# Modulation multiply-adds on VectorE: directly behind each step's weight residue instead of at the step's end

## The reference

```python
def modulation(cvec, w, b):
    return jnp.split(jax.nn.silu(cvec) @ w + b, 6, axis=-1)

    mx = modulation(c, ada_w[i], ada_b[i])
    mc = modulation(c_ctx, ada_w[i], ada_b[i])
    hx = modulate(rms_norm(x, norm_g[i, 0]), mx[0][:, None], mx[1][:, None])
...
    x = x + mx[2][:, None] * yx
    hx = modulate(rms_norm(x, norm_g[i, 1]), mx[3][:, None], mx[4][:, None])
...
    x = x + mx[5][:, None] * y[:b * s].reshape(b, s, d)
```

## Time and profile before

| | |
|---|---|
| median of 3 runs | 2205.7 us (2204.92 to 2208.37) |
| profiled execution, device time | 2208.73 us |
| its span, first to last instruction | 2207.2 us |
| TensorE busy (matmul) | 1989.5 us (90%) |
| VectorE busy | 1227.8 us (56%) |
| ScalarE busy | 496.2 us (22%) |
| mean granted TensorE clock | 0.956 of full |
| group 0, about | 136 to 236 us |
| groups 1 to 7, about | 236 to 1003 us |
| output projection, routing | 1003 to 1270 us |
| experts | 1270 to 2207 us |

### The profile page before, as it was taken

How to read it: one execution, slowest core, us unless ns; L and a number is a source line. 1 busy time by engine, 2 the same in 40 slices (tenths; PEclk the granted TensorE clock), 3 DMA queues, 4 the chain that set the end, 5 groups by cost and what they waited for, 6 DMA issues and landing times.

```text
span 2207.2 us, 27594 instructions
## 1 busy us (share of the span) xinstructions
PE 1989.5 (90%) x10090; PEld 1232.7 (56%) x10090; DVE 1227.8 (56%) x1999; ACT 496.2 (22%) x577; POOL 152.3 (7%) x214
## 2 busy tenths in 40 slices
PE   5778999999999999998999798998988999888988
PEld 2357777788787878786778533333333333333333
DVE  2456788888888888887786623332223333322224
ACT  3123333333333333334445300000000000000000
POOL 0000000000000000000592100000000000000000
PEclk9788999999999999999999899999999999999999
DMA  9958576767676767678663699999999999999997
GB/s 351 311 172 241 161 220 182 221 182 221 183 219 186 215 192 215 188 224 298 209 210 133 243 423 426 428 427 426 425 427 425 427 426 427 427 425 426 426 425 286
DMA packets 294717, 666.68 MB, mean 302 GB/s; under 512 B 13504, under 2 KB 188000, under 8 KB 261008
## 3 DMA queue, kind: packets, MB, share of 16 engines
q1 hardware_dynamic: 285728, 639.45, 77.6%
q0 software_dynamic: 7984, 26.40, 3.6%
q10 hardware_dynamic: 960, 0.23, 0.1%
HBM read 655.40 MB, written 10.65 MB: 302 GB/s over the span
## 4 chain that ended last, share of the span: by engine, by line
DMA 29%; PE 20%; SPq 1%; DVE 1%; issue 1%; ACT 0%; DVEq 0%
DMA wt<-in_moe_w_up 28%; PE bank L1826 12%; PE bank L1683 5%; PE bank L1851 1%; SPq L527 1%; SPq L520 1%; PE bank L1790 0%; PE bank L1791 0%; DMA raw<-in_ssm_w_out 0%; PE bank L1742 0%; PE bank L1808 0%; DVE wlo L961 0%; PE bank L1783 0%; PE bank L1735 0%; DVE x L1460 0%
## 5 line engine op out<-in xcount | busy, mean ns | idle before, releaser
L1826 PE MATMUL bank<-wt,xe 128*64 128x512 f32 x1984 | 465.7, 624 | 82.8 <-DMA wt<-in_moe_w_up 82.8
L1460 DVE TENSOR_TENSOR x<-x,bank 128x512 f32<-128x512 f32 x256 | 158.5, 681 | 536.1 <-PE bank L1808 536.1
L1580 PE MATMUL bank<-hTh,whi 128*128 128x256 f32 (+1 forms) x1264 | 409.1, 344 | 16.2 <-ACT whi L704 13.8
L1581 PE MATMUL bank<-hTl,whi 128*128 128x256 f32 (+1 forms) x1264 | 402.0, 338 | 0.0
L1826 PEld LDWEIGHTS bank<-wt,xe 128*64 128x64 f32 x1984 | 163.8, 143 | 381.5 <-issue 381.5
L1580 PEld LDWEIGHTS bank<-hTh,whi 128*128 128x128 f32 x1264 | 242.4, 192 | 48.1 <-ACT whi L704 15.5
L1581 PEld LDWEIGHTS bank<-hTl,whi 128*128 128x128 f32 x1264 | 242.5, 192 | 23.9
L1585 PE MATMUL bank<-hTh,wlo 128*128 128x256 f32 (+1 forms) x1264 | 236.1, 340 | 20.6 <-DVE wlo L951 20.6
L1851 PE MATMUL bank<-wt,hdn 128*64 128x512 f32 x1024 | 226.8, 595 | 1.4 <-DVE hdn L1472 1.4
L1585 PEld LDWEIGHTS bank<-hTh,wlo 128*128 128x128 f32 x1264 | 199.9, 194 | 47.1 <-DVE wlo L951 22.9
L704 ACT ACTIVATE whi<-raw 128x2048 fp32r<-128x2048 f32 x80 | 153.1, 1913 | 303.8 <-DMA raw<-in_ssm_w_in 301.6
(11 more groups left out here) (304 smaller groups left out, 1836.1 us busy)
## 6 DMA issues: line engine op xcount, KB each, us to landing
wt<-in_moe_w_gate SPq DMA_DIRECT2D x64, 2048.0 KB, 16.7
wt<-in_moe_w_up SPq DMA_DIRECT2D x64, 2048.0 KB, 21.1
wt<-in_moe_w_down SPq DMA_DIRECT2D x64, 2048.0 KB, 18.5
raw<-in_ssm_w_in SPq DMA_DIRECT2D x80, 1024.0 KB, 6.1
raw<-in_ada_w SPq DMA_DIRECT2D x70, 1024.0 KB, 6.2
raw<-in_ssm_w_out SPq DMA_DIRECT2D x32, 1024.0 KB, 5.1
fr<-in_ada_w SPq DMA_DIRECT2D x26, 1024.0 KB, 11.5
bc<-cum_d POOLq DMA_DIRECT2D x32, 512.0 KB, 4.8
```

What stands on the lines that cost most here:

```text
L1460: dve.tensor_tensor(x1[:, tt, cols], x1[:, tt, cols], banks[(1, 3, 6, 7)[nb]][:, :], ALU.add).then_inc(s_acc2, 1)
L1580: pe.matmul(bank[:, 0:width], wh[:, k, :], hTh[:, k, 0:width], start=(k == 0), stop=False)
L1581: last = pe.matmul(bank[:, 0:width], wh[:, k, :], hTl[:, k, 0:width], start=False, stop=False)
L1826: last = pe.matmul(banks[0][SLOTS * h:SLOTS * h + SLOTS, :], rows[:, k, :], wt[2 * q + h][:, FF * i:FF * i + FF], start=(k == 0), stop=(k ...
```

## The change

`ada_sum` is called directly behind `conv_lo` in VectorE's step and no longer at its end. No operation, size, buffer or semaphore changes, and no other engine's code.

```diff
@@ -1144,6 +1144,8 @@
                         differences(s, 1)
                     if w and n + 1 < NCH and not (isinstance(g, int) and g == 0 and n < 2):
                         conv_lo(g, n + 1)
+                    if w and n in ADA_STEP:
+                        ada_sum(g, ADA_STEP[n])
                     if w and n + 1 == NCH:
                         if not (isinstance(g, int) and g == GROUPS - 1):
                             conv_lo(g + 1, 0)
@@ -1205,8 +1207,6 @@
                         ada_columns(g, 1)
                     if ssd and w and n == 1:
                         weights(s, 0)
-                    if w and n in ADA_STEP:
-                        ada_sum(g, ADA_STEP[n])
 
             def ada_sum(g, j):
 
```

## The result

| | before | after |
|---|---|---|
| median of 4 runs each | 2205.53 us (2204.92 to 2208.37) | 2225.41 us (2224.01 to 2226.95) |
| ratio of the medians | | 1.0096, 95% interval 1.0084 to 1.0108 |
| profiled execution, device time | 2208.73 us | 2224.4 us |
| its span | 2207.2 us | 2222.9 us |
| mean granted clock | 0.956 | 0.955 |

The kernel became slower by 19.9 us by the medians and by 15.7 us between the two profiled executions. The forecast was 2218.5 us, in a range of 2211 to 2231. Its direction and range held, and its +12.8 us was 7 us short of the gap of the medians.

A forecast was written before the change was run, and what follows sets the result against it. VectorE's chain, ending two TensorE stalls, was taken to bound each group: 2.76 + 0.5 - 1.01 = +2.25 us, times seven +15.8, less 3.0 in the first group, +12.8. Forecast 2218.5 us, range 2211 to 2231.

The forecast's parts named there:

- What bounds a group: In the seven full groups, two TensorE stalls end with VectorE instructions, so VectorE's chain up to them sets what changes.
- The view by occupancy: Rival: busier TensorE absorbs VectorE's shift in the seven groups; only the first group changes, -3.0 us, 2203 us; chance 0.08.
- Tile 4, +2.76 a group: Step 5: its sum now precedes half 1's weights, so TensorE's y products of heads 4 to 7 start 2.76 us later.
- Tile 0, +0.5 a group: Step 0: its sum delays differences and ScalarE's exponentials, so VectorE waits 0.5 us for chunk 2's rounded weights.
- Tiles 1 and 2, -1.01 a group: Step 3: tile 1's earlier sum frees the slot for chunk 4's weights sooner, removing VectorE's 1.01 us wait.
- (b): Sums may wait for their tile's load, tightest tile 3, 7.0 us after issue: 0 to 2 us late, taken as 0.
- (c): Tile 4's sum may wait for TensorE's column sums of the first half: 0, up to 1 us if TensorE is late.
- the rival of the larger loss: Late tile loads and column sums cost some 1 us more a group: +20 to +25 us, 2226 to 2231; chance 0.12.
- The first group, -3.0: Tile 2's earlier sum frees the slot for chunk 5's weights, removing TensorE's 2.23 us wait and 1.2 us clock loss.
- the clock behind B: TensorE's clock after its stall before the y products of heads 4 to 7: extra loss 0, at most 0.4 us a group.
- upper bound of 3.8 us a group: Highest loss allowed for each of the seven groups, against a lowest of 1.7; together +9 to +24 us in all.
- The rival that it becomes faster: VectorE's 2.75 and 1.26 us waits in steps 4 and 5 are late weights that earlier loads remove: 2190 us; chance 0.07.

The follow-up runs named there:

- e8: The changed kernel with tile 0 summed behind the first differences, tile 3 behind chunk 5's residue in step 4, tile 4 back at its step's end: 2154.67 us.
- e1: The changed kernel with only tile 4's sum put back at its step's end: 2199.78 us.
- e3: The changed kernel with the sums of tiles 0 and 4 put back at their steps' ends: 2194.97 us.
- e5: The kernel before with only the sums of tiles 1 and 2 moved early: 2194.77 us.
- the second pair: Second profiles of the two unchanged kernels, e9 (before) and e10 (after): spans 2204.0 and 2221.8 us.
- e6: The kernel before with an unused VectorE sum, 1.48 us of delay, ahead of the weights of half 1: 2218.96 us.
- e7: The kernel before with a longer unused VectorE sum, 5.48 us of delay, ahead of the weights of half 1: 2247.91 us.
- e9: The kernel before, unchanged, run again for a second profile: 2205.59 us, one run.
- e4: The kernel before with only tile 0's sum moved early: 2209.54 us.
- e2: The kernel before with only tile 4's sum moved early: 2229.81 us.
- e10: The changed kernel, unchanged, run again for a second profile: 2223.34 us, one run.

## Why the prediction was right, and which term was mis-sized

**What bounds a group.** Right. The time of the group loop follows VectorE's position at two points, although TensorE is the busier engine. TensorE is busy with the same 10090 matmuls in after and e8 alike; the order on VectorE, with no operation added, moved the time from 2154.7 to 2229.8 us. The view by occupancy, by which only the first group would have changed (2203 us), falls.

**Tile 4, +2.76 a group.** Right: the stall went from 2.35 to 5.07 us, and E to B from 73.81 in e1 to 76.56 in after.

**Tile 0, +0.5 a group.** Right: a wait of 0.53 us stands at the residue of chunk 2, and e3 to e1 differ by 0.6 us from E to B.

**Tiles 1 and 2, -1.01 a group.** Right: the wait is gone, and E to B is 73.2 in e5 against 74.4 and 74.5 in the two profiles of before. That is 0.2 to 0.3 more than forecast; in both profiles of before the second group takes 0.7 to 1.6 us longer than the other early ones, which is part of it and which no run explains. Together with the two terms above: forecast +2.25 from E to B, measured +2.15 and, in the second pair, +2.1.

**Bounds (b) and (c), tiles waited for.** Both were 0, as taken. Tile 3, priced as the tightest at 7.0 us from issue to use, was issued at 606.94 and summed at 613.81 with no wait, 6.9 us later:

```profile
606.94 0.37 SPq L481 DMA_DIRECT2D raw<-in_ada_w  x1
```

Tile 4's sum at 634.32 has no wait for TensorE's column sums, which had started at 630.90. So the rival of the larger loss, built on these, did not happen.

**The first group, -3.0.** The mechanism was right, but only about half of the gain is there in every execution. TensorE's 2.23 us wait for chunk 5's weights turned into this, in the timeline of after:

```profile
183.19 0.69 DVE L994 SCALAR_TENSOR_TENSOR slx<-slx,cv 128x512 f32<-128x512 f32 x1
...
183.93 0.66 PE L1608 MATMUL bank<-ident,slx 128*128 128x128 f32 x4 [0.59 <-DVE slx L994]
```

From its first projection to E the first group took 95.0 to 95.7 us in the seven profiles in which tile 2 is early. In the six others it depends on how long TensorE waits for chunk 5's weights: 98.4 to 98.8 us behind waits of 2.1 to 2.4 us, with the clock down to 0.63 to 0.69 over the 4 us that follow (before, e6, e7), and 96.8 to 97.0 behind waits of 1.4 to 1.7 us, with the clock at 1.00 (e9, e4, e2). So the move is worth some 1.6 us where the wait is short and 3.3 where it is long and takes the clock too: 3.5 us between the first two profiles and 1.3 in the second pair, against 3.0 forecast.

**The step that was mis-sized: the clock behind B, taken as 0 with 0.4 us a group as its upper end.** It measured +0.66 us a group in the first pair of profiles and +1.1 in the second (35.68 against a mean of 34.54), both above the upper end. The prediction argued that the loss behind B was already paid in before, because one profiled execution, 3 us slower than the median, showed a clock of 0.59 in the group it read. Two things were wrong with that. The price was not always paid: behind a stall of 2.3 us, 20 groups of 48 kept the full clock. And 0.59 over 3.6 us was not the floor: behind 3.7 us or more most stretches are at 0.50, and none at 1.00. With the second pair's values the sum is 7 x (2.1 + 1.1) = 22.4 less 1.3 for the first group, so 21; with the first pair's it is 7 x (2.15 + 0.66) = 19.7 less 3.5, so 16; 19.9 was measured. How much of it a given pair shows depends on how often the kernel before happened to lose its clock.

That the time stayed inside the range was partly luck. The 0.4 us a group that was allowed for the clock reaches only to 7 x (2.25 + 0.4) - 3.0 = 15.6 us, 2221.3. (The upper bound of 3.8 us a group is not the sum of its own terms, 2.25 + 0.4 + 2 + 1 = 5.65; it was a choice between them.) The rest of the range, up to 2231, was room for late tiles and late column sums, (b) and (c), and these measured 0; the clock used that room. That its loss has an upper end, as e7 shows, kept it from needing more.

**The rival that it becomes faster.** It supposed that the waits of 2.75 and 1.26 us were late loads. They are the same in after, 2.74 and 1.27, though weights are loaded sooner: ScalarE's waits for them in the groups fell from the first of these lines (before, 236 to 1003 us) to the second (after, 236 to 1020 us),

```profile
ACT whi L704 <- DMA raw<-in_ssm_w_in: 265.9, 45, 10.1
...
ACT whi L704 <- DMA raw<-in_ssm_w_in: 26.9, 9, 4.1
```

and e8 shows what does remove the 2.75: work of VectorE's own in its place.

## What to carry to other kernels

In an engine that works in order, ask of each piece of filler work which instruction of the same engine stands behind it and who waits for that. Put filler behind the instruction that another engine waits for, into the hole in which your engine waits for the answer; ahead of it, the filler moves the hole and fills nothing. Judge a mixed move piece by piece: here two tiles of eight gained 10 to 11 us, one cost 24 to 26, and one 4 to 5. And before a loss is called already paid, look at it in a second profile of the same kernel.

## What the runs showed of the hardware

The clock behind a short idle time of TensorE varies between executions of one program: behind 2.3 us it stayed at 1.00 (20 groups of 48) or fell to between 0.53 and 0.68 over 3.6 us; what decides it was not found. Behind 3.7, 5.1 and 7.7 us it always fell, mostly to 0.50, and B to E was longer than the 34.2 us at full clock by the same 1.4 to 1.5 us in the mean, whatever the length of the stall. In after and e10 the stretch grows from group to group, 34.8 to 36.2 us, in the same steps in both, because the granted clock over the 8 us behind B goes from 0.82 to 0.65; why the low stretch shifts against B in this way was not tried. Where TensorE had no gap, in e8, the granted clock was 1.00 over a whole group of 102 us.
